# Two layers and a routed block on one core: norm factors applied at the products' exit

## The chip, the cores and the metric

The kernel runs on one core of a Trainium2 chip, as one program. The metric is device microseconds of that core for the whole program, the median of several runs; smaller is better. TensorE multiplies, VectorE and ScalarE prepare its operands and take its results out of PSUM, GpSimd does part of the expert stage, and SyncE's queue issues the transfers of weights.

## What is computed

The input is x, 512 tokens by 1024, and all is fp32. Two layers are followed by a second block:

```python
for l in range(2):
    x = x + 0.5 * swiglu(rmsnorm(x, ffn1_norm[l]), w_gate, w_up, w_down)
    h = rmsnorm(x, mix_norm[l])
    parts = split(h @ w_in[l])
    o = concat(mla_attention(...), nsa_attention(...), stick_breaking_attention(...))
    x = x + o @ w_out[l]
    x = x + 0.5 * swiglu(rmsnorm(x, ffn2_norm[l]), w_gate, w_up, w_down)
x = rmsnorm(x, final_norm)
hn = rms_norm(x, attn_norm_g)
h = x + (sigmoid(ga) * (gmlp(u, v) @ w_proj_a) + sigmoid(gb) * (swa(q, k, v) @ w_proj_b)) @ w_out
h = h + hierarchical_moe(rms_norm(h, ffn_norm_g), ...)   # 16 experts, two for each token
out = rms_norm(h, final_norm_g)
```

`rmsnorm(x, g)` is x · g · rstd, with rstd = (mean of x² over the 1024 features + eps)^(−1/2), one factor for each token. `swiglu` is (silu(h w_gate) · (h w_up)) w_down with 2816 inner columns, silu(a) = a · sigmoid(a).

## The kernel before

**Layout and products.** x stays on chip transposed, `x_T`: 8 chunks (`KC`) of 128 features by 512 tokens. Each matrix product is done in split form: an operand is rounded to a high part (`..._hi`, ScalarE) and the remainder is its low part (`..._lo`, VectorE), and hi·hi, lo·hi and hi·lo are summed in PSUM. One such product is 128 × 128 by 512 columns.

**Feed-forward parts** (`slices`, two in each layer). The 2816 inner columns go in `NSL` = 11 slices of 256. In a slice TensorE does the gate half (48 products, into `score[0:2]`), the up half (48, `score[2:4]`) and the down part of an earlier slice (8 chunks `c` of 6 products, into two banks `acc[c % 2]` in turn), whose results VectorE adds to `x_T`. The weights of each half go through `split_weights(l, ph, w, sl)` on ScalarE and then on VectorE, w = 0 for gate, 1 for up, 2 for down. The gate half is turned into silu by ScalarE's Exp of −a and VectorE's add of 1, reciprocal and product (`gate`); `hidden` multiplies by the up half and splits the result. The last slice's down weights are put into the gate weights' tiles (`tile=0`).

**Norms** (`norm` on TensorE and ScalarE, `square_sum` and `norm_split` on VectorE). As each chunk of x becomes final (`x_final`), ScalarE squares it into `h_T` and VectorE sums the squares. Two fp32 products with a matrix of ones sum over the partitions (`ssq_full`). ScalarE computes rstd with Ln and Exp, VectorE writes x · gain · rstd into `h_T`, ScalarE makes its high part and VectorE its low part, chunk by chunk. Then the first products of the next stage can run.

**Mixer** (`mix`). A list of tickets `MIX` (name, number, weight load, evacuating engine) sets the order; each has one product group from `acc[n % 2]`, and the engine in the list takes the result out. After the attentions come the tickets of the output product: p0 to p7 (first 768 rows of w_out), then q0 to q7 (last 256 rows, unsplit fp32), whose results VectorE adds to x. Loads of weights share three slots in turn; a load is issued when the last ticket that uses its slot is done (`LAST_TICKET`), and the next part's gate weights take slot 0.

**Second block.** Its own norm (`norm_both`), then tickets `SEC_T`: u, v, wst (transposes of the spatial weights), q, k, values, the sliding window attention with half of a gate ticket in each step, and so on to the router. **Experts** (`step`, `x_pass`): for each of 16, ScalarE makes the high parts, VectorE the low parts of the gate and up weights in two pieces each (`xg_lo`, `xu_lo`) and of the expert's gathered tokens (`mine_lo`), and GpSimd those of the down weights (`xd_lo`, line 2682). TensorE does gate, up and an earlier expert's down half in turn.

Each engine works through its own instructions in the order in which the code writes them; an instruction that waits holds up all behind it on its engine.

## Time and profile before

| | |
|---|---|
| time, median of 3 runs | 3158.56 us (3156.81 to 3162.05) |
| profiled execution | 3159.24 us |
| its span | 3157.4 us |
| mean granted TensorE clock | 0.965 |
| TensorE busy | 2927.1 us, 93% |
| VectorE busy | 2042.9 us, 65% |
| ScalarE busy | 1136.5 us, 36% |
| GpSimd busy | 217.3 us, 7% |

The span is that of one profiled execution; the times of the runs are taken without a profile. A timeline row has its start, its duration, engine, line, operation, output and inputs, and in brackets how long the engine stood idle before it and what ended that. Rows with "x2" are two instructions taken together. A matrix product's duration of 0.39 us is that at the granted clock of 2.4 GHz, 0.63 and more at 1.2 GHz; the starts of such products in a run lie closer than their durations, since they overlap.

### The profile page before, as it was taken

What the parts mean: (1) busy time and instruction counts of PE and PEld (TensorE: products, weight loads), DVE (VectorE), ACT (ScalarE), POOL (GpSimd) and SP (SyncE); (2) the same over time, 40 slices, a digit from 0 to 9 for tenths busy, and PEclk for the clock granted to TensorE, in tenths of its full rate; (3) what the DMA queues carried; (4) which work ended last, traced back from release to release, by engine and by line L of the source; (5) the groups of instructions that cost most, each with busy time, mean ns of one, the idle gap of its engine ahead of it and who ended that gap; (6) DMA issues with size and microseconds to landing.
All of it is one profiled execution on the core that took longest, in us unless ns stands there. A gap on an engine that the chain in (4) does not pass through costs nothing. (4 is left out here: it accounts for less than half of the span.)

```text
span 3157.4 us, 36951 instructions
## 1 busy us (share of the span) xinstructions
PE 2927.1 (93%) x13178; PEld 2257.2 (71%) x13178; DVE 2042.9 (65%) x2675; ACT 1136.5 (36%) x1658; POOL 217.3 (7%) x68
## 2 busy tenths in 40 slices
PE   5999989999899998999989999899997999978885
PEld 3888868566588886888767566588876767667774
DVE  5677742675577777777733774677776544467876
ACT  3212132467321213221132566322114333256674
POOL 0000000000000000000000000000000000046663
PEclk8999999999999999999999999999998889989998
DMA  6323223000232322232232000323214112368995
GB/s 160 107 93 99 89 63 75 31 1 24 80 107 93 102 84 81 93 106 93 78 75 63 21 1 24 107 93 106 93 40 116 55 43 79 132 229 319 326 337 195
DMA packets 234685, 324.56 MB, mean 103 GB/s; under 512 B 58720, under 2 KB 202088, under 8 KB 222144
## 3 DMA queue, kind: packets, MB, share of 16 engines
q1 hardware_dynamic: 228400, 309.88, 30.3%
q0 software_dynamic: 5584, 11.02, 1.3%
q10 hardware_dynamic: 576, 2.10, 0.2%
q8 instruction: 65, 1.06, 0.1%
q14 instruction: 60, 0.49, 0.0%
...
## 5 line engine op out<-in xcount | busy, mean ns | idle before, releaser
L2024 DVE SCALAR_TENSOR_TENSOR x_T<-acc,x_T 128x512 f32<-128x512 f32 x352 | 242.9, 691 | 205.3 <-PE acc L929 205.3
L898 PE MATMUL score<-h_hi,gate_hi 128*128 128x512 f32 x704 | 280.2, 398 | 41.5 <-DVE h_lo L1978 32.5
L2004 DVE RECIPROCAL recip_tile<-exp_tile 128x512 f32<-128x512 f32 x88 | 295.1, 3353 | 7.2 <-issue 0.9
L899 PE MATMUL score<-h_lo,gate_hi 128*128 128x512 f32 x704 | 278.4, 396 | 0.0
L900 PE MATMUL score<-h_hi,gate_lo 128*128 128x512 f32 x704 | 278.2, 395 | 0.0
L898 PE MATMUL score<-h_hi,up_hi 128*128 128x512 f32 x704 | 274.6, 390 | 0.1
L900 PE MATMUL score<-h_hi,up_lo 128*128 128x512 f32 x704 | 274.2, 390 | 0.0
L899 PE MATMUL score<-h_lo,up_hi 128*128 128x512 f32 x704 | 274.2, 390 | 0.0
L927 PE MATMUL acc<-hid_hi,down_hi 128*128 128x512 f32 x640 | 251.9, 394 | 8.8 <-DVE x_T L2024 8.8
L928 PE MATMUL acc<-hid_lo,down_hi 128*128 128x512 f32 x640 | 252.0, 394 | 0.0
L929 PE MATMUL acc<-hid_hi,down_lo 128*128 128x512 f32 x640 | 251.9, 394 | 0.0
L1514 ACT ACTIVATE up_hi<-weights 128x2048 fp32r<-128x2048 f32 x44 | 84.4, 1918 | 311.0 <-PE score L900 310.0
L1514 ACT ACTIVATE down_hi<-weights 128x2048 fp32r<-128x2048 f32 x40 | 76.7, 1917 | 327.3 <-PE acc L929 326.8
L898 PEld LDWEIGHTS score<-h_hi,gate_hi 128*128 128x128 f32 x704 | 135.1, 192 | 76.0 <-DVE h_lo L1978 37.2
L1592 ACT ACTIVATE exp_tile<-score 128x512 f32<-128x512 f32 x88 | 47.8, 595 | 367.9 <-PE score L900 367.9
L2667 POOL DMA_DIRECT2D arena<-rel_scratch x1 | 1.0, 964 | 2375.9 <-PE acc L1252 2375.9
L2569 DVE TENSOR_TENSOR xg_lo<-arena,xg_hi 128x2048 fp32r<-128x2048 f32 x32 | 127.8, 4024 | 50.6 <-ACT xg_hi L1854 50.6
L899 PEld LDWEIGHTS score<-h_lo,gate_hi 128*128 128x128 f32 x704 | 135.2, 192 | 28.1
L900 PEld LDWEIGHTS score<-h_hi,gate_lo 128*128 128x128 f32 x704 | 134.8, 191 | 28.5
L2682 POOL TENSOR_TENSOR xd_lo<-weights,xd_hi 128x2048 fp32r<-128x2048 f32 x30 | 154.2, 5163 | 5.7 <-ACT xd_hi L1854 5.3
L898 PEld LDWEIGHTS score<-h_hi,up_hi 128*128 128x128 f32 x704 | 132.2, 188 | 28.7 <-issue 0.9
L899 PEld LDWEIGHTS score<-h_lo,up_hi 128*128 128x128 f32 x704 | 132.2, 188 | 27.3
...
## 6 DMA issues: line engine op xcount, KB each, us to landing
...
```

What stands on the lines that cost most here:

```text
L898: mm(ps, hi[:, kc, cols], h_hi[:, kc, :], start=kc == 0, stop=False, skip_group_check=True)
L899: mm(ps, hi[:, kc, cols], h_lo[:, kc, :], start=False, stop=False, skip_group_check=True)
L900: return mm(ps, lo[:, kc, cols], h_hi[:, kc, :], start=False, stop=kc == KC - 1, skip_group_check=True)
L927: mm(acc[c % 2][:, :], hi[:, j, cols], hid_hi[:, 2 * par + j, :], start=j == 0, stop=False)
L928: mm(acc[c % 2][:, :], hi[:, j, cols], hid_lo[:, 2 * par + j, :], start=False, stop=False)
L929: m = mm(acc[c % 2][:, :], lo[:, j, cols], hid_hi[:, 2 * par + j, :], start=False, stop=j == 1)
L1514: fn(w_hi[tile][:, :], slot[w][:, :], ACT.Copy).then_inc(w_hi_ready[w], 1)
L1592: fn(et[:, c, :], score[c][:, :], ACT.Exp, scale=-1.0).then_inc(sig_ready, 1)
L2004: V.reciprocal(rt[:, :], et[:, c, :])
L2024: V.scalar_tensor_tensor(x_T[:, c, :], acc[c % 2][:, :], 0.5, x_T[:, c, :], ALU.mult, ALU.add).then_inc(acc_free[c % 2], 1)
L2569: V.tensor_tensor(x_lo[t][j][:, :], x_raw[t][j], x_hi[t][j][:, :], ALU.subtract).then_inc(x_lo_ready[t], 1)
L2682: nc.gpsimd.tensor_tensor(x_lo["d"][j][:, :], x_raw["d"][j], x_hi["d"][j][:, :], ALU.subtract).then_inc(x_lo_ready["d"], 1)
```

## The change

1. **Norm factors at the exit.** In both layers the split is made of x · gain (`enter` on ScalarE, `low` on VectorE), with no rstd in it. The rstd of a token is multiplied in when a product leaves PSUM: in `gate` two products by rstd (`gated`), and two more (`gated2`) that carry the up half's factor; in the mixer in the evacuations, which for that move from ScalarE to VectorE, and for the two by-token kinds (vsw, sv) with a transposed copy `rstd_T`.
2. **Square sums behind products.** VectorE adds the squares up (`add_squares`), and TensorE's products with ones (`sum_squares`) stand between gate and up half of slice 0, and in the mixer ahead of the second ticket.
3. **Tangent for the sigmoid.** ScalarE computes tanh(a/2), VectorE (tanh + 1) · gated2; the factor of down becomes 0.25. The reciprocals go, and `gate_taken` is given after the first two products by rstd.
4. **Reorderings.** (a) The loads of w_out change slots, q's with p's last, so that slot 0 is free after p7, and the gate weights of the second part are split ahead of the q adds. (b) wst comes first in the second block. (c) The sliding window's half gate products come one step earlier. (d) In the experts `mine_lo` comes between the two `xg_lo`. Besides, the last slice's down weights go into the tiles of gate or up (`tile=ph`) and wait until the last up half is done, and the mixer's first weights are split ahead of the last adds of the first part.

```diff
-    [("cq", 0, 0, "act"), ("cq", 1, 0, "act"), ("ckv", 0, 1, "act"), ("kr", 0, 1, "act")]
...
+    [("cq", 0, 0, "dve"), ("cq", 1, 0, "dve"), ("ckv", 0, 1, "dve"), ("kr", 0, 1, "dve")]
...
+    + [("sq", 0, 7, "dve"), ("rope", 10, None, "dve"), ("sq", 1, 7, "dve"), ("xs_v", 0, None, "act")]
...
-for _n in range(W_OUT0, W_OUT0 + 4):
-    LAST_TICKET[_n] = OUT_T["p", 2 * (_n - W_OUT0) + 1]
-LAST_TICKET[W_OUT0 + 4] = OUT_T["q", KC - 1]
+P_LOAD, Q_LOAD = (14, 15, 16, 18), 17
+for _j, _n in enumerate(P_LOAD):
+    LAST_TICKET[_n] = OUT_T["p", 2 * _j + 1]
+LAST_TICKET[Q_LOAD] = OUT_T["q", KC - 1]
...
-        SEC_T = ([("u", c, c // 2) for c in range(4)]
+        SEC_T = ([("wst", b, None) for b in range(2)]
+                 + [("u", c, c // 2) for c in range(4)]
                  + [("v", b, 2 + b // 2) for b in range(4)]
-                 + [("wst", b, None) for b in range(2)]
...
+            def sum_squares(k, sq, n_direct):
+
+                for c in range(KC - n_direct, KC):
+                    pe.wait_ge(squared, k * KC + c + 1)
+                    mm(turn[0][:, :], cst("ones"), sq[c], start=c == KC - n_direct, stop=False)
...
                 pe.wait_ge(summed, k + 1)
-                mm(turn[0][:, :], cst("ones"), h_T[:, 0, :], start=True, stop=False)
-                pe.wait_ge(squared, k * KC + KC)
-                mm(turn[0][:, :], cst("ones"), h_T[:, KC - 1, :], start=False, stop=True).then_inc(ssq_full, 1)
+                mm(turn[0][:, :], cst("ones"), sums, start=False, stop=True).then_inc(ssq_full, 1)
...
                     half(sl, 0)
+                    if isinstance(sl, int) and sl == 0:
+                        sum_squares(l * 3 + 2 * ph, ffn_sq, 1)
                     half(sl, 1)
...
-                    tile = 0 if last else 2
+                    tile = ph if last else 2
...
+                    if (name, i) == ("cq", 1):
+                        sum_squares(l * 3 + 1, mix_sq, 2)
+                    if (name, i) == ("nq", 1):
+                        pe.wait_ge(rstd_ready, l * 3 + 2)
+                        for b in range(TB):
+                            m = nc.tensor.transpose(turn[1][:, b * P:(b + 1) * P], rstd[:, b * P:(b + 1) * P], ident)
+                        m.then_inc(rstd_turned, 1)
...
+                half_gate(0)
...
-                    g = n // 2
-                    linear2(T2["gate", g], "gate", g, 7 + g // 2, range(4 * (n % 2), 4 * (n % 2) + 4))
+                    if n + 1 < NSW:
+                        half_gate(n + 1)
...
+            def row_scale(k):
+
                 act.wait_ge(ssq_full, k + 1)
                 fn(rstd[:, :], turn[0][:, :], ACT.Ln, scale=1.0 / D, bias=eps[:, :])
                 act.drain()
                 fn(rstd[:, :], rstd[:, :], ACT.Exp, scale=-0.5).then_inc(rstd_ready, 1)
...
+            def enter(k, sq, hi):
+
+                for c in range(KC):
+                    act.wait_ge(x_final, k * KC + c + 1)
+                    fn(hi[:, c, :], x_T[:, c, :], ACT.Copy, scale=gains[:, bass.ds(k, 1), c:c + 1][:, 0, :]
+                       ).then_inc(h_hi_ready, 1)
+                    fn(sq[c], x_T[:, c, :], ACT.Square).then_inc(squared, 1)
...
+                    if not later:
+                        row_scale(l * 3 + 2 * ph)
                     act.wait_ge(hid_done, at(l, TG, gub + sl * 2 + 2))
-                    act.wait_ge(gu_full, gu_at(l, gub, sl * 2 + 1))
+                    act.wait_ge(gate_taken, slices_at(l, ph, sl + 1))
                     for c in range(2):
-                        fn(et[:, c, :], score[c][:, :], ACT.Exp, scale=-1.0).then_inc(sig_ready, 1)
+                        fn(et[:, c, :], gated[c], ACT.Tanh, scale=0.5).then_inc(sig_ready, 1)
...
-                split_weights(l, ph, 2, NSL - 1, tile=0)
+                act.wait_ge(gu_full, gu_at(l, gub, 2 * NSL))
+                split_weights(l, ph, 2, NSL - 1, tile=ph)
...
-                norm(l * 3 + 1, mix=l)
+                split_mix(l, 0)
+                enter(l * 3 + 1, mix_sq, mix_h[0])
                 mix(l)
-                norm(l * 3 + 2, (l, 1))
+                split_weights(l, 1, 0, 0)
+                enter(l * 3 + 2, ffn_sq, h_hi)
...
+            def low(l, nth, c):
+
+                hi, lo = mix_h if nth == 1 else (h_hi, h_lo)
+                dve.wait_ge(h_hi_ready, at(l, 3 * KC, nth * KC + c + 1))
+                V.scalar_tensor_tensor(lo[:, c, :], x_T[:, c, :], gains[:, bass.ds(l * 3 + nth, 1), c:c + 1][:, 0, :],
+                                       hi[:, c, :], ALU.mult, ALU.subtract).then_inc(h_split, 1)
+
+            def add_squares(k, sq, n, out=sums):
+
+                dve.wait_ge(squared, k * KC + n)
+                m = V.tensor_tensor(out, sq[0], sq[1], ALU.add)
+                for c in range(2, n):
                     dve.drain()
-                    dve.wait_ge(h_hi_ready, at(l, 3 * KC, nth * KC + c + 1))
-                    V.tensor_tensor(lo[:, c, :], h_T[:, c, :], hi[:, c, :], ALU.subtract).then_inc(h_split, 1)
-
-                if ph is None:
-                    split_mix(l, 0)
-                else:
-                    split_weights(l, ph, 0, 0)
-                dve.wait_ge(rstd_ready, k + 1)
-                for c in range(KC):
-                    V.scalar_tensor_tensor(h_T[:, c, :], x_T[:, c, :], gains[:, bass.ds(k, 1), c:c + 1][:, 0, :],
-                                           rstd[:, :], ALU.mult, ALU.mult).then_inc(h_ready, 1)
-                    if c >= 1:
-                        low(c - 1)
-                low(KC - 1)
-                if ph is None:
-                    split_mix(l, 1)
-
-            def slices(l, ph, k):
+                    m = V.tensor_tensor(out, out, sq[c], ALU.add)
+                m.then_inc(summed, 1)
...
+                    if isinstance(sl, int) and sl == 0:
+                        dve.wait_ge(rstd_ready, l * 3 + 2 * ph + 1)
+                    dve.wait_ge(gu_full, gu_at(l, gub, sl * 2 + 1))
                     for c in range(2):
+                        m = V.tensor_tensor(gated[c], score[c][:, :], rstd[:, :], ALU.mult)
+                    m.then_inc(gate_taken, 1)
+                    dve.drain()
+                    for c in range(2):
+                        V.tensor_tensor(gated2[c], gated[c], rstd[:, :], ALU.mult)
+                    for c in range(2):
+                        dve.drain()
                         dve.wait_ge(sig_ready, at(l, TG, gub + sl * 2 + c + 1))
-                        V.tensor_scalar(et[:, c, :], et[:, c, :], 1.0, None, ALU.add)
-                        dve.drain()
-                        V.reciprocal(rt[:, :], et[:, c, :])
-                        dve.drain()
-                        m = V.tensor_tensor(et[:, c, :], rt[:, :], score[c][:, :], ALU.mult)
-                    m.then_inc(gate_taken, 1)
+                        V.scalar_tensor_tensor(et[:, c, :], et[:, c, :], 1.0, gated2[c], ALU.add, ALU.mult)
...
-                        V.scalar_tensor_tensor(x_T[:, c, :], acc[c % 2][:, :], 0.5, x_T[:, c, :],
+                        V.scalar_tensor_tensor(x_T[:, c, :], acc[c % 2][:, :], 0.25, x_T[:, c, :],
...
                         if last:
                             dve.drain().then_inc(x_final, 1)
-                            square_sum(k, c - 1)
+                            if ph == 0 and c >= 1:
+                                low(l, 1, c - 1)
...
-                split_weights(l, ph, 2, NSL - 1, tile=0)
+                split_weights(l, ph, 2, NSL - 1, tile=ph)
...
+                if ph == 0:
+                    split_mix(l, 0)
                 down(NSL - 1, True)
...
             def mix(l):
+                low(l, 1, KC - 1)
+                add_squares(l * 3 + 1, mix_sq, KC - 2)
+                split_mix(l, 1)
...
+                    if (name, i) == ("cq", 0):
+                        dve.wait_ge(rstd_ready, l * 3 + 2)
+                    if who == "dve" and (name, i) in EVAC:
+                        t, sc = EVAC[name, i]
+                        r = t.shape[0]
+                        V.scalar_tensor_tensor(t, ps[0:r, :], sc, rstd[0:r, :], ALU.mult, ALU.mult
+                                               ).then_inc(acc_free[n % 2], 1)
...
+                split_weights(l, 1, 0, 0)
                 dve.drain()
                 for c in range(KC):
                     add_out("q", c)
                     dve.drain().then_inc(x_final, 1)
-                    square_sum(l * 3 + 2, c - 1)
+                    if c >= 1:
+                        low(l, 2, c - 1)
+                low(l, 2, KC - 1)
+                add_squares(l * 3 + 2, ffn_sq, KC - 1)
...
-                    split_x("g", n + 1)
+                    split_x("g", n + 1, (0,))
                     mine_split(n + 1, 1 - q)
+                    split_x("g", n + 1, (1,))
```

VectorE at the end of the first feed-forward part, before: the hidden split of the last slice, adds to x of the two last down parts (L2024), sums of squares into h_T (L1953), then the mixer's first weight split.

```order
L2014 TENSOR_TENSOR exp_tile<-exp_tile,score 128x512 x2
L2016 CAST hid_hi<-exp_tile 128x1024
L2018 TENSOR_TENSOR hid_lo<-exp_tile,hid_hi 128x1024
...
L2024 SCALAR_TENSOR_TENSOR x_T<-acc,x_T 128x512
...
L2024 SCALAR_TENSOR_TENSOR x_T<-acc,x_T 128x512
...
L1953 TENSOR_TENSOR h_T<-h_T 128x512
...
L2024 SCALAR_TENSOR_TENSOR x_T<-acc,x_T 128x512
...
L1967 TENSOR_TENSOR mix_w_lo_62<-weights,mix_w_hi_61 128x2048
```

The same place after. L2066 is the add to x, L2012 the mixer's weight split, L2019 the low part of x · gain, L2025 and L2028 the sums of squares.

```order
L2056 TENSOR_TENSOR exp_tile<-exp_tile,score 128x512 x2
L2058 CAST hid_hi<-exp_tile 128x1024
L2060 TENSOR_TENSOR hid_lo<-exp_tile,hid_hi 128x1024
...
L2066 SCALAR_TENSOR_TENSOR x_T<-acc,x_T 128x512
...
L2012 TENSOR_TENSOR mix_w_lo_62<-weights,mix_w_hi_61 128x2048
...
L2066 SCALAR_TENSOR_TENSOR x_T<-acc,x_T 128x512
...
L2019 SCALAR_TENSOR_TENSOR mix_h_lo<-x_T,gains,mix_h_hi 128x512
...
L2066 SCALAR_TENSOR_TENSOR x_T<-acc,x_T 128x512
...
L2025 TENSOR_TENSOR probs_T<-arena 128x512
L2028 TENSOR_TENSOR probs_T<-probs_T,arena 128x512 x4
```

The weight split has moved ahead of the last eight adds, the low parts between them, and the sums behind them.

VectorE in the q tickets of the mixer, before: the last p add, q adds (L2215), sums of squares, and behind them the split of the second part's gate weights (L1961) and the norm.

```order
L2215 TENSOR_TENSOR x_T<-acc,x_T 128x512
...
L2215 TENSOR_TENSOR x_T<-acc,x_T 128x512
...
L1953 TENSOR_TENSOR h_T<-h_T 128x512
...
L2215 TENSOR_TENSOR x_T<-acc,x_T 128x512
...
L1961 TENSOR_TENSOR gate_lo<-weights,gate_hi 128x2048
...
L1986 SCALAR_TENSOR_TENSOR h_T<-x_T,gains,rstd 128x512
...
L1978 TENSOR_TENSOR h_lo<-h_T,h_hi 128x512
```

The same place after.

```order
L2271 TENSOR_TENSOR x_T<-acc,x_T 128x512
...
L2006 TENSOR_TENSOR gate_lo<-weights,gate_hi 128x2048
...
L2271 TENSOR_TENSOR x_T<-acc,x_T 128x512
...
L2019 SCALAR_TENSOR_TENSOR h_lo<-x_T,gains,h_hi 128x512
...
L2271 TENSOR_TENSOR x_T<-acc,x_T 128x512
...
L2025 TENSOR_TENSOR probs_T<-h_T 128x512
L2028 TENSOR_TENSOR probs_T<-probs_T,h_T 128x512 x5
```

The split of gate_lo now stands between the last p add and the first q add, and low parts follow each q add.

VectorE in one expert's step, before.

```order
L2569 TENSOR_TENSOR xg_lo_65<-arena,xg_hi_71 128x2048
...
L2569 TENSOR_TENSOR xg_lo_66<-arena,xg_hi_72 128x2048
L2576 TENSOR_TENSOR mine_lo_79<-turn,mine_hi_77 128x512 x2
L2593 SCALAR_TENSOR_TENSOR probs<-recip_tile,score 128x512
...
L2596 SCALAR_TENSOR_TENSOR probs<-probs,score 128x512
L2569 TENSOR_TENSOR xu_lo_67<-arena,xu_hi_73 128x2048
```

The same step after.

```order
L2636 TENSOR_TENSOR xg_lo_65<-arena,xg_hi_71 128x2048
L2643 TENSOR_TENSOR mine_lo_79<-turn,mine_hi_77 128x512
...
L2636 TENSOR_TENSOR xg_lo_66<-arena,xg_hi_72 128x2048
L2661 SCALAR_TENSOR_TENSOR probs<-recip_tile,score 128x512
...
L2664 SCALAR_TENSOR_TENSOR probs<-probs,score 128x512
L2636 TENSOR_TENSOR xu_lo_67<-arena,xu_hi_73 128x2048
```

The second xg_lo has moved behind mine_lo; the rest stands as it did.

## Rows read from the trace of the kernel before

**Rows 1.** The page, part 1: busy us, share of the span, instructions.

```profile
PE 2927.1 (93%) x13178; PEld 2257.2 (71%) x13178; DVE 2042.9 (65%) x2675; ACT 1136.5 (36%) x1658; POOL 217.3 (7%) x68
```

**Rows 2.** The page, part 5: line, operation, count, busy us, mean ns, idle before.

```profile
L2004 DVE RECIPROCAL recip_tile<-exp_tile 128x512 f32<-128x512 f32 x88 | 295.1, 3353 | 7.2 <-issue 0.9
```

**Rows 3.** Timeline of TensorE: start us, us, line, operands, [idle before, its releaser].

```profile
72.11 0.79 PE L898 MATMUL score<-h_hi,gate_hi 128*128 128x512 f32 x1 [5.57 <-DVE gate_lo L1961]
...
400.85 0.50 PE L927 MATMUL acc<-hid_hi,down_hi 128*128 128x512 f32 x1 [2.19 <-DVE x_T L2024]
...
418.80 1.92 PE L878 MATMUL turn<-h_T,const 128*128 128x512 f32 x2 [2.25 <-DVE h_T L1953]
...
427.60 0.80 PE L949 MATMUL acc<-mix_h_hi,mix_w_hi 128*128 128x512 f32 x1 [5.18 <-DVE mix_h_lo L1978]
...
438.38 0.39 PE L949 MATMUL acc<-mix_h_hi,mix_w_hi 128*128 128x512 f32 x1
438.61 0.40 PE L949 MATMUL acc<-mix_h_lo,mix_w_hi 128*128 128x512 f32 x1
...
825.93 1.13 PE L878 MATMUL turn<-h_T,const 128*128 128x512 f32 x2 [1.68 <-DVE h_T L1953]
...
837.93 0.80 PE L898 MATMUL score<-h_hi,gate_hi 128*128 128x512 f32 x1 [10.02 <-DVE h_lo L1978]
...
863.37 0.49 PE L898 MATMUL score<-h_hi,gate_hi 128*128 128x512 f32 x1 [1.19 <-DVE gate_lo L1961]
...
1216.35 0.80 PE L898 MATMUL score<-h_hi,gate_hi 128*128 128x512 f32 x1 [5.20 <-DVE h_lo L1978]
...
2392.74 0.77 PE L1252 MATMUL acc<-mix_h_hi,sec_hi 128*128 128x512 f32 x1 [13.82 <-DVE mix_h_lo L2344]
...
2449.14 0.80 PE L1252 MATMUL acc<-mix_h_hi,sec_hi 128*128 128x512 f32 x1 [5.19 <-DVE exp_tile L2493]
...
2494.93 1.22 PE L1306 MATMUL score<-arena 64*128 64x256 f32 x2 [4.06 <-DVE stats L2436]
...
2952.45 0.49 PE L1417 MATMUL score<-xg_hi,mine_hi 128*128 128x512 f32 x1 [2.25 <-DVE mine_lo L2576]
```

**Rows 4.** Timeline of VectorE, end of the first feed-forward part and mixer.

```profile
389.40 2.29 DVE L1961 TENSOR_TENSOR gate_lo<-weights,gate_hi 128x2048 fp32r<-128x2048 f32 x1
...
391.89 0.69 DVE L2024 SCALAR_TENSOR_TENSOR x_T<-acc,x_T 128x512 f32<-128x512 f32 x1 [0.20 <-PE acc L929]
...
430.51 0.74 DVE L1986 SCALAR_TENSOR_TENSOR h_T<-x_T,gains,rstd 128x512 f32<-128x512 f32 x1
...
514.07 2.08 DVE L2159 SCALAR_TENSOR_TENSOR lora<-lora,lora_gains,exp_tile 128x512 f32<-128x512 f32 x3
```

**Rows 5.** Timeline of ScalarE, first norm of the mixer, gate weights of the second part.

```profile
422.46 0.69 ACT L1562 ACTIVATE rstd<-turn,eps 128x512 f32<-128x512 f32 x1 [0.80 <-PE turn L880]
...
424.50 0.63 ACT L1564 ACTIVATE rstd<-rstd 128x512 f32<-128x512 f32 x1
...
829.57 1.91 ACT L1514 ACTIVATE gate_hi<-weights 128x2048 fp32r<-128x2048 f32 x1 [3.89 <-DMA weights<-in_ffn_w_gate]
```

**Rows 6.** Windows in the mixer: stretch, us, busy of PE, PEld, DVE, ACT, POOL, clock, DMA.

```profile
480.00:525.00 45.00, 43.64 (x240) 36.30 (x239) 15.62 (x15) 18.50 (x21) 0.00 (x0) 1.00 0.44 94
```

**Rows 7.** Timeline of VectorE, one expert.

```profile
2942.62 8.49 DVE L2569 TENSOR_TENSOR xg_lo<-arena,xg_hi 128x2048 fp32r<-128x2048 f32 x2 [3.03 <-ACT xg_hi L1854]
...
2951.03 1.28 DVE L2576 TENSOR_TENSOR mine_lo<-turn,mine_hi 128x512 fp32r<-128x512 f32 x2
...
2953.68 4.49 DVE L2569 TENSOR_TENSOR xu_lo<-arena,xu_hi 128x2048 fp32r<-128x2048 f32 x2
```

**Rows 8.** Timeline of GpSimd, two experts.

```profile
2936.40 10.36 POOL L2682 TENSOR_TENSOR xd_lo<-weights,xd_hi 128x2048 fp32r<-128x2048 f32 x2
...
2956.86 5.78 POOL L2682 TENSOR_TENSOR xd_lo<-weights,xd_hi 128x2048 fp32r<-128x2048 f32 x1
```

**Rows 9.** Line 2682 on GpSimd: duration ns min/median/max.

```profile
L2682 POOL TENSOR_TENSOR xd_lo<-weights,xd_hi x30: 4595/4633/6666, 2809.1 to 3106.5; 128x2048 fp32r<-128x2048 f32 x30
```

142 lines of the change are left out of this document (79 added, 63 removed).

## The prediction, made before the changed kernel had run

> **What bounds the kernel now.** I read the page's busy shares first: TensorE is busy for 2927.1 of 3157.4 us [rows 1]. Whatever does not take away an idle stretch of TensorE, or put work into one, moves nothing. So the second view is TensorE's timeline, and in it the rows that end an idle stretch [rows 3]. They stand where one stage hands over to the next: at each norm, at the end of each feed-forward part, in the second block's first steps, and once for each expert. The third view is the timelines of VectorE and ScalarE at these places [rows 4, 5], to see which instruction ends each wait and what is queued ahead of it. The last views are VectorE's and GpSimd's timelines in the experts [rows 7 to 9]. The sum is made against the profiled execution's own 3159.24 us, which lies 0.7 above the median of 3158.56.
>
> **What frees an engine but not the path.** The tangent takes away 88 reciprocals of 3.35 us, 295 us of VectorE [rows 2]. VectorE is at 65% [rows 1]. Inside the slices TensorE does not wait for it, so I book 0. The cover is the next slice's split weights, which are ready some 9 us before they are used: VectorE's split of gate_lo starts at 389.40 [rows 4], and in every slice comes ahead of eight down chunks of 1.36 us.
>
> **Start.** The first products come about 3 us sooner, since no norm precedes them. But TensorE then stops again where it stops now, at 72.11, for gate weights whose transfer the change does not touch [rows 3]. 0, bounds ±1.5.
>
> **First feed-forward part into the mixer (twice).** Before, the last down product ends at 418.80 − 2.25 = 416.55. The two square-sum products, the Ln and the Exp (422.46 to 425.13 [rows 5], with a table load between them), and gain and factor on VectorE lie before 427.60. The first ticket then runs at 1.2 GHz (0.80 us a record against 0.39 at 438.38) and waits chunk by chunk; the second ticket begins at 438.38 [rows 3]. After the change, new things come first. The last down weights are split only when the up half of the last slice is done, so ScalarE's 1.9 and VectorE's 2.29 stand ahead of the add that now starts at 391.89 [rows 4]: +2.3. The mixer's first weight split (2.29) is put ahead of the last adds, where TensorE has two banks of 1.36 of cover: +1.0. VectorE then needs about 1.56 per chunk (add 0.69, the low part 0.75 [rows 4], a drain) against TensorE's 1.36: +0.9. So down ends at 420.8, and the first ticket follows without a wait, 24 products 0.227 apart (438.38, 438.61 [rows 3]) = 5.4, to 426.2. Three fp32 products of 0.86 (the pair at 825.93 takes 1.13 with its run-out [rows 3]) bring it to 428.8. The chain of squares (last low part, five adds of 0.69) ends near 426.4 and is covered with little to spare. 438.4 − 428.8 = 9.6 saved, bounds 7 to 12, twice: **−19.2**.
>
> **Inside the mixer.** Fifteen evacuations per layer go from ScalarE (0.60) to VectorE (0.75, as the row with gain and factor [rows 4]). TensorE has two banks and tickets of some 5.5 us, and VectorE is busy for only 15.6 of 45 us there [rows 6]. Only the one behind the short gate ticket is late: VectorE is in the lora products until 516.15 [rows 4], so that the ticket after next starts some 1.55 later. Four transposes add 0.6, and one wait of 0.5 goes. 1.65 twice: **+3.3**, bounds 1 to 6.
>
> **Mixer into the second feed-forward part (twice).** Before, the gate weights could be requested only behind the last q chunk (825.93 − 1.68 = 824.2) and their ScalarE split starts at 829.57 [rows 3, 5], 5.3 later; TensorE starts at 837.93 after 10.02 idle. Now they are requested when p7 is done, at 810.5, and land at 815.9; ScalarE has its part at 817.8 and VectorE at 820.1. But VectorE's split is written ahead of all q adds, so the two banks are full at 813.9 and TensorE stands until 820.9: a **new wait of 7.0**. Six q chunks of 1.72 follow, some 3 us slower since the clock falls in such a gap as it does at 427.60. q ends at 834.2, and the gate half starts at once. At full clock (10.9, and 1.7 for two square products) the up half begins at 846.8, where it now begins at 851.0. The wait of 1.19 at 863.37 [rows 3], behind VectorE's reciprocals, goes too. 5.4 twice: **−10.8**. Bounds: 0, if the new wait costs all that it hides, and 8.
>
> **Second feed-forward part into layer 1.** The same late split (+2.3). The norm's 11.1 us between down and gate half become 3.9 of low parts and gate_lo, and two square products of 1.7 inside. The slow start after the 5.20 at 1216.35 [rows 3] shrinks by 1, and slice 1 no longer waits (1.2). **−4.6**, bounds 2 to 7.
>
> **Into the second block.** Its norm stays; the wait of 13.82 at 2392.74 [rows 3] hangs on weights requested after the last x, so it follows the late split: +1.6. The spatial transposes (1.35) move into it, with the 5.19 wait at 2449.14 that they caused [rows 3], and the slow ticket behind that wait gets 2.1 back: **−7.0**, bounds 4 to 9.
>
> **Sliding window.** Half a gate product (12 products, 2.75) is moved into the wait of 4.06 at 2494.93 [rows 3], and part of the slow clock with it goes: −4.7, +0.4 at the next ticket: **−4.3**, bounds 1 to 6.
>
> **Experts.** TensorE idles 2.25 before nearly each gate half, released by mine_lo [rows 3]. The change puts mine_lo ahead of the second xg_lo (2.28), which looks like −2.2 for each of 15 experts, −33. The rows speak against it. xg_lo's pair takes 8.49 where two of 2.28 would take 4.6 [rows 7]: the first starts at 2942.62, while GpSimd's xd_lo runs until 2946.76 [rows 8], and ends 2.15 after that. GpSimd's pair takes 10.36 [rows 8] where two of the median 4.63 [rows 9] would take 9.3: it is issued at 2956.86, and VectorE's xu_lo pair runs until 2958.17 [rows 7]. The two engines exclude each other, and their turns form a ring: from the end of xd_lo VectorE needs 11.4 (xg_lo twice, mine_lo, two short ones, xu_lo twice, 2946.76 to 2958.17 [rows 7]), then GpSimd 9.2, together 20.5; the two xd_lo starts lie 20.46 apart [rows 8]. The change only permutes three members of this ring. TensorE starts each gate half 2.2 sooner and waits 2 us longer for xd_lo in the down half: **0**, bounds ±4: the longest xd_lo took 6.7 [rows 9], 2 us lost in the ring, and two such may come or go.
>
> The Trainium skill's page "SBUF — State Buffer", section "Who interferes with whom", says that a VectorE instruction with two SBUF inputs and a GpSimd one that reads SBUF hold a shared port by an exclusive lock, the later one blocked for the whole of the earlier. By that rule the experts give 0; by a mere sharing of bandwidth they would give up to −33. The trace agrees with the rule: 2.15 us after xd_lo's end is one whole xg_lo.
>
> **Sum.** 0 − 19.2 + 3.3 − 10.8 − 4.6 − 7.0 − 4.3 + 0 = −42.6. 3159.24 − 42.6 = 3116.6, and 0.7 less on the median: **3116**. All the favourable bounds together give −67, the others −10.
>
> **The rivals.** (1) *New waits eat the gain.* The 7.0 before the q adds saves nothing, and each of the four late down splits costs 4.6 and not 2.3, as TensorE falls to the lower clock behind them: −42.6 + 10.8 + 9.2 = −22.6, 3136; with the mixer's bound, 3139. For it: the idle of 7.0 is longer than the 5.18 after which the clock is low at 427.60 [rows 3]. Against: weights and q adds have nothing else ahead of them. (2) *The ring in the experts opens.* If xu_lo and xd_lo interleave so that VectorE's 2.7 us of unlocked work hides behind GpSimd, each cycle falls towards TensorE's own 18.2 (20.46 − 2.25): up to −33, about 3083. Against: 11.4 and 9.2 make up the 20.46 to 0.2 us, and the order of xu_lo and xd_lo is not changed. (3) *Slower than before: VectorE becomes the mixer's exit.* If each of the 30 moved evacuations stands behind a weight split of 2.29 when its bank is needed, the mixer costs 68.7 instead of 3.3: −45.9 + 68.7 = +23, 3181. It is slower than before from 1.7 us each. Against: a late evacuation costs only what exceeds the second bank's 5.5 us, and VectorE is one third busy there [rows 6]. (4) *The change does not do what it says:* the sum products wait on TensorE for squares that come too late (they lie 2 us ahead), so that TensorE stands between first and second ticket, as now before the first. The three norm terms (−34.6) go and what they had absorbed (4.2 twice, 2.3) stays: −42.6 + 34.6 + 10.7 = +2.7, 3161, no change.
>
> **How the numbers follow.** Forecast, 3092 to 3140 with rival 1's smaller forms: 0.80. Rival 1 beyond 3140: 0.07. Rival 2 below 3092: 0.04. Rival 4, within 0.2% (6.3 us, about what a measurement of this kernel can tell from none): 0.04. Rival 3 and like ones, slower: 0.05. Faster by more than 0.2%: 0.91, same 0.04, slower 0.05. The range is that of the 0.80.
>
> **What would show it.** In the trace after: no idle before the first mixer ticket, and the second beginning some 9.6 us sooner counted from the end of the up half of the last slice; a new wait near 7 us in the q chunks with gate_lo as releaser, and none before the gate half; in the experts still 20.5 between xd_lo pairs, with TensorE's wait moved from mine_lo to xd_lo. A ring below 20 would prove the experts' step wrong; waits at mixer tickets released by VectorE's evacuations, of more than 1 us and more than two a layer, would prove the mixer's.

## The result, and the profile after

The changed kernel takes 3127.02 us, the median of four runs (3123.23 to 3128.6), against 3158.18 for the kernel before in the same session: a ratio of 0.9898 (95% interval 0.9882 to 0.9914), 31.2 us less. The forecast was 3116, with a range from 3092 to 3140. In a second session it took 3129.42, and the kernel before 3161.63 (0.9906, 0.9891 to 0.9921). Its profiled execution took 3123.23 and is the shortest of its four runs; its span is 36.0 below that of before.

The page of the changed kernel, head and part 1:

```profile
span 3121.4 us, 36929 instructions
...
PE 2920.3 (94%) x13194; PEld 2256.0 (72%) x13194; DVE 1825.3 (58%) x2653; ACT 1121.3 (36%) x1638; POOL 212.4 (7%) x68
```

TensorE's idle time fell from 230 to 201 us; VectorE lost 218 us of work. The timeline of TensorE after, rows that end an idle stretch or begin a stage:

```profile
395.12 0.50 PE L940 MATMUL acc<-hid_hi,down_hi 128*128 128x512 f32 x1 [2.30 <-DVE x_T L2066]
...
420.32 0.49 PE L962 MATMUL acc<-mix_h_hi,mix_w_hi 128*128 128x512 f32 x1
...
425.90 1.88 PE L889 MATMUL turn<-arena,const 128*128 128x512 f32 x4
...
428.07 0.79 PE L962 MATMUL acc<-mix_h_hi,mix_w_hi 128*128 128x512 f32 x1
...
507.18 0.50 PE L962 MATMUL acc<-mix_h_hi,mix_w_hi 128*128 128x512 f32 x1 [1.82 <-DVE arena L2199]
...
813.18 12.68 PE L954 MATMUL acc<-o_T,weights 128*128 128x512 f32 x24 [7.09 <-DVE x_T L2271]
...
1200.33 0.79 PE L909 MATMUL score<-h_hi,gate_hi 128*128 128x512 f32 x1 [6.89 <-DVE h_lo L2019]
...
2366.76 0.77 PE L1271 MATMUL acc<-mix_h_hi,sec_hi 128*128 128x512 f32 x1 [11.11 <-DVE mix_h_lo L2412]
```

These answer to [rows 3]. 420.32 is the first mixer ticket: the waits of 2.25 and 5.18 at 418.80 and 427.60 are gone, and 428.07 is the second ticket, which began at 438.38. Its first record overlaps the sums ahead of it, so the table below goes by its second product (428.70 after, 438.61 before). 395.12 and 813.18 are the two waits that the prediction added (2.3 and 7.0 forecast, 2.30 and 7.09 found). 1200.33 answers to the row at 1216.35, and its wait has grown from 5.20 to 6.89. At 2366.76 the second block's wait is 11.11 where it was 13.82, since the spatial transposes and two more products with ones fill part of it.

Where the 36.0 us of the two profiled executions lie, read at the same instruction of TensorE in both timelines (start after minus start before, and the difference between neighbouring places):

| place | ahead of before by | this stretch | forecast |
|---|---|---|---|
| up to the first part's last down products | 0.4 | −0.4 | 0 |
| mixer's second ticket, layer 0 | 9.9 | −9.5 | −9.6 |
| first q chunk, layer 0 | 7.9 | +2.0 | +1.65 |
| slice 1 of the second part, layer 0 | 14.1 | −6.2 | −5.4 |
| slice 1 of the first part, layer 1 | 16.7 | −2.6 | −4.6 |
| mixer's second ticket, layer 1 | 25.9 | −9.2 | −9.6 |
| first q chunk, layer 1 | 21.6 | +4.3 | +1.65 |
| slice 1 of the second part, layer 1 | 27.8 | −6.2 | −5.4 |
| first row of the sliding window | 34.7 | −7.0 | −7.0 |
| first expert's gate half | 39.9 | −5.2 | −4.3 |
| end | 36.0 | +3.9 | 0 |

### The profile page after: what moved, and what is told of

Same layout as the page of the kernel before. It is cut to its first block, busy times and chain, and to the rows that moved or that the text cites. A ratio compares the mean times of both kernels' runs of the same rounds, so it can differ in the third digit from the quotient of the medians.

```text
span 3121.4 us, 36929 instructions
## 1 busy us (share of the span) xinstructions
PE 2920.3 (94%) x13194; PEld 2256.0 (72%) x13194; DVE 1825.3 (58%) x2653; ACT 1121.3 (36%) x1638; POOL 212.4 (7%) x68
## 4 chain that ended last, share of the span: by engine, by line
PE 83%; DVE 4%; DMA 3%; issue 2%; ACT 2%; POOL 2%; DVEq 1%; SPq 1%; ACTq 0%; POOLq 0%
PE score L909 10%; PE score L911 10%; PE score L910 10%; PE acc L1271 8%; PE acc L962 6%; PE acc L940 5%; PE acc L942 5%; PE acc L941 5%; PE score L996 4%; PE acc L1017 4%; PE score L1444 3%; POOL xd_lo L2750 2%; PE acc L1444 2%; PE acc L954 2%; DMA weights<-in_ffn_w_gate 1%
## 5 line engine op out<-in xcount | busy, mean ns | idle before, releaser
L2066 DVE SCALAR_TENSOR_TENSOR x_T<-acc,x_T 128x512 f32<-128x512 f32 x352 | 242.4, 691 | 402.8 <-PE acc L942 402.4
L909 PE MATMUL score<-h_hi,gate_hi 128*128 128x512 f32 x704 | 277.7, 394 | 22.1 <-DVE h_lo L2019 14.1
L1620 ACT ACTIVATE exp_tile<-probs 128x512 f32<-128x512 f32 x88 | 50.8, 625 | 409.1 <-DVE probs L2041 409.1
L940 PEld LDWEIGHTS acc<-hid_hi,down_hi 128*128 128x128 f32 x640 | 120.9, 189 | 46.3 <-DVE x_T L2066 21.3
```

The lines of the kernel that those rows point to most:

```text
L909: mm(ps, hi[:, kc, cols], h_hi[:, kc, :], start=kc == 0, stop=False, skip_group_check=True)
L940: mm(acc[c % 2][:, :], hi[:, j, cols], hid_hi[:, 2 * par + j, :], start=j == 0, stop=False)
L2066: V.scalar_tensor_tensor(x_T[:, c, :], acc[c % 2][:, :], 0.25, x_T[:, c, :], ALU.mult, ALU.add).then_inc(acc_free[c % 2], 1)
```

## The experiments

Each kernel was timed against the kernel before on the same chip. "−n" is the median's distance from that kernel's. "Less than the changed kernel" goes by the median of the changed kernel's second session, 3129.42.

**The changed kernel again (`a0_after`).** No edit.

> The changed kernel once more, unaltered, as the measure for the runs beside it. Its profiled execution was 36.0 us below that of the kernel before, the medians 31.2 apart. Expected: 3127 again, within 3; where two executions differ, the difference should lie in the experts (from about 2746 us to the end), where the distance between two pairs of xd_lo is irregular (19.3 to 22.5), and not ahead of them.

Measured 3129.42 (3125.8 to 3134.5), −32.2. Its trace is 0.35 ahead of the first one's at the start, loses 2.2 more than that one in layer 0's mixer, stays 2.2 to 2.5 behind up to the experts and ends 2.6 behind. So the difference lies in the mixer and not, as I had expected, in the experts (+4.1 here, +3.9 there, though their pairs of xd_lo lie differently); more on that below.

**The experts' order undone (`e1_moe_undo`).**

```diff
-                    split_x("g", n + 1, (0,))
+                    split_x("g", n + 1)
                     mine_split(n + 1, 1 - q)
-                    split_x("g", n + 1, (1,))
```

> The changed kernel with the experts' order as before (both xg_lo, then mine_lo). Theory of the ring (VectorE's and GpSimd's instructions exclude each other, and their turns set the distance of 20.5): the reordering gains nothing and by the traces loses 3 to 4 us (39.9 us ahead at the first expert's gate half, 36.0 at the end), so this kernel takes 3122 to 3125. Rival (TensorE's wait on mine_lo was the bound, and the reordering saves what it moves): this kernel is slower than the changed one by 5 to 30.

Measured 3124.76 (3123.43 to 3128.06), −36.9, ratio 0.9889 (0.9874 to 0.9904) where the changed kernel has 0.9906 (0.9891 to 0.9921). The medians are 4.7 apart in the forecast direction, with overlapping intervals. The rival that the reordering saves 5 to 30 us falls. The traces say less than the medians: from the first gate half to the end this kernel is 4.1 longer than before, which has the same order there, and the changed one 3.9 and 4.1 in its two traces. So the 3.9 can't be put down to the order. The length of this stage differs without any edit in it: with the old order it is 3.1 longer than before in `f1_tanh_only` and 0.1 in `f2_wst_half`, with the new order 6.4 in `e2_gatelo_late` and 8.1 in `e5_unroll`. What the reordering costs by itself lies between nothing and 5 us; it was not settled. That it gains nothing by itself is shown.

**An expert's two products ahead of the first xg_lo (`e3_probs_first`).**

```diff
+                dve.wait_ge(xsig_ready, n + 1)
+                V.scalar_tensor_tensor(xhid, sig, 1.0, score[q][:, :], ALU.add, ALU.mult)
+                dve.drain()
+                dve.wait_ge(x_used["u"], n * 2 + 4)
+                V.scalar_tensor_tensor(xhid, xhid, 0.5, score[2 + q][:, :], ALU.mult, ALU.mult).then_inc(xhid_ready, 1)
                 if last is None:
                     split_x("g", n + 1, (0,))
...
-                dve.wait_ge(xsig_ready, n + 1)
```

> The changed kernel with VectorE's two products of one expert's gate and up results (0.67 and 0.69, with 0.15 between) moved ahead of the first xg_lo. They read PSUM, so that they can run while GpSimd does xd_lo. Theory of the ring: 1.5 us less in each of 14 rounds of it, 21 in all, so 3106, with 19.0 between xd_lo pairs. Rival (transfers bound this stage; their engines are 0.9 busy at some 330 GB/s): within 5 of the changed kernel. Second rival: VectorE waits there for the up half, misses xd_lo's end, and it is slower by up to 10.

Measured 3111.42 (3105.94 to 3112.88), −50.2: 18.0 less than the changed kernel beside it. GpSimd's timeline in it:

```profile
2914.63 9.18 POOL L2750 TENSOR_TENSOR xd_lo<-weights,xd_hi 128x2048 fp32r<-128x2048 f32 x2
...
2934.67 9.18 POOL L2750 TENSOR_TENSOR xd_lo<-weights,xd_hi 128x2048 fp32r<-128x2048 f32 x2
...
2954.71 4.63 POOL L2750 TENSOR_TENSOR xd_lo<-weights,xd_hi 128x2048 fp32r<-128x2048 f32 x1
```

The distance of pairs (from end to end), 20.5 or 21.5 in eleven of the fourteen rounds of the kernel before, is 20.0 to 20.1 in eleven and 19.0 in the last three. The forecast was 19.0, and 21 us in all. GpSimd's gather is now what stands between: it ends 0.9 after xu_lo, so that a round is 10.0 of VectorE, 0.9 and 9.2 of xd_lo.

**The same edit on the kernel before (`f3_before_probs`).**

> The kernel before with one change alone: VectorE's two products of an expert's gate and up results ahead of the first xg_lo. Theory of the ring: its rounds of 20.5 and 21.5 (20.8 on average) become 20.0, so 11 to 18 less than before, by the experts alone, with no other stage touched. Rival: the gain of e3 came from the place of mine_lo in it, and this kernel gains under 4.

Measured 3159.28 (3157.02 to 3165.35), ratio 1.0001 (0.9992 to 1.001): no gain at all. Here my theory of the ring fell short: it had VectorE's splits and GpSimd's xd_lo in it, but not the two indirect transfers that GpSimd issues ahead of each xd_lo: the store of an expert's result (L2686) and the gather of a later expert's tokens (L2674). Two rounds of this kernel, VectorE, then GpSimd, then TensorE:

```profile
2973.51 4.48 DVE L2569 TENSOR_TENSOR xu_lo<-arena,xu_hi 128x2048 fp32r<-128x2048 f32 x2
...
2987.09 0.69 DVE L2593 SCALAR_TENSOR_TENSOR probs<-probs,score 128x512 f32<-128x512 f32 x1 [3.56 <-PE score L1417]
...
2993.55 4.48 DVE L2569 TENSOR_TENSOR xu_lo<-arena,xu_hi 128x2048 fp32r<-128x2048 f32 x2
```

```profile
2974.81 1.87 POOL L2686 DMA_INDIRECT expert_scratch<-exp_tile,slot_ids  x1 [6.78 <-ACT exp_tile L1871]
2976.98 1.88 POOL L2674 DMA_INDIRECT lora<-h_scratch,slot_ids  x1 [0.31 <-issue]
2978.88 9.19 POOL L2682 TENSOR_TENSOR xd_lo<-weights,xd_hi 128x2048 fp32r<-128x2048 f32 x2
2996.13 2.78 POOL L2686 DMA_INDIRECT expert_scratch<-probs_T,slot_ids  x1 [8.06 <-ACT probs_T L1871]
2999.22 1.00 POOL L2674 DMA_INDIRECT lora<-h_scratch,slot_ids  x1 [0.30 <-issue]
3000.24 9.20 POOL L2682 TENSOR_TENSOR xd_lo<-weights,xd_hi 128x2048 fp32r<-128x2048 f32 x2
```

```profile
2973.73 0.49 PE L1417 MATMUL score<-xg_hi,mine_hi 128*128 128x512 f32 x1 [2.59 <-DVE mine_lo L2576]
...
2993.76 0.49 PE L1417 MATMUL score<-xg_hi,mine_hi 128*128 128x512 f32 x1 [0.22 <-DVE mine_lo L2576]
```

The product at 2987.09 waits for the up half (idle 3.56, released by TensorE), so VectorE's row of instructions now hangs on TensorE too. Still the pace is that of the ring through GpSimd. From the end of xd_lo at 2968.02 VectorE needs 10.0 up to the end of xu_lo (2977.99), where it needed 11.4 before. The gather ends 0.9 later, xd_lo takes 9.2: together 20.1. In the next round, from 2988.07, the store starts later against xu_lo. Now it is the store that ends 0.9 after xu_lo (2998.03 and 2998.91), and the gather comes on top with 1.3: 21.4. The pairs lie 20.1 and 21.4 apart by turns, where they lay 20.5 and 21.5 apart in most rounds of the kernel before. So the two issues ate most of the 1.5 that the move took off VectorE, and two rounds of 23.0 and 23.4 ate the rest.

The same place in the kernel with both edits (`e3_probs_first`), VectorE, then GpSimd's store and gather:

```profile
2898.97 0.69 DVE L2660 SCALAR_TENSOR_TENSOR probs<-probs,score 128x512 f32<-128x512 f32 x1 [1.72 <-PE score L1444]
...
2899.57 6.36 DVE L2636 TENSOR_TENSOR xg_lo<-arena,xg_hi 128x2048 fp32r<-128x2048 f32 x1
...
2905.85 1.28 DVE L2643 TENSOR_TENSOR mine_lo<-turn,mine_hi 128x512 fp32r<-128x512 f32 x2
...
2907.05 2.27 DVE L2636 TENSOR_TENSOR xg_lo<-arena,xg_hi 128x2048 fp32r<-128x2048 f32 x1
```

```profile
2909.90 2.52 POOL L2754 DMA_INDIRECT expert_scratch<-probs_T,slot_ids  x1 [6.13 <-ACT probs_T L1916]
2912.72 1.89 POOL L2742 DMA_INDIRECT lora<-h_scratch,slot_ids  x1 [0.30 <-issue]
```

Here mine_lo ends at 2907.13, ahead of the second xg_lo, and the gate half starts 3.5 after the end of xd_lo, not 5.7. The down half ends 3.1 after it in all rounds but the first, as in the short rounds of `f3_before_probs`; in the long ones there it ends 5.3 to 5.5 after it. The store waits until ScalarE has taken out the down half, and in this kernel it is always early enough. This points to a way from mine_lo's place to GpSimd through TensorE. ScalarE's queue, which waits for weights as well, stands between the two, and what share it has in the store's moment was not tested. By the medians, the reordering in the change is worth nothing alone, the two products' move is worth nothing alone, and together they take 18 us.

**The gate weights' split behind q6 (`e2_gatelo_late`).**

```diff
-                split_weights(l, 1, 0, 0)
                 dve.drain()
                 for c in range(KC):
+                    if c == 7:
+                        split_weights(l, 1, 0, 0)
                     add_out("q", c)
```

> The changed kernel with VectorE's split of the second part's first gate weights between the q6 and q7 adds, not ahead of q0's. Theory (the new wait of 7.1 at the q chunks is only the price of that place): q chunks run without a stop, the split ends near 817.5 where the gate half now starts at 825.3, so 7 to 8 us less in each layer, 3112. Rival (ScalarE's and VectorE's work chunk by chunk or the lower clock behind the norm sets the start of the gate half): less than 3 in each layer.

Measured 3119.5 (3117.45 to 3122.52), −42.1, 9.9 less than the changed kernel. Slice 1 of the second part starts 9.7 ahead of before, counted from the first q chunk, in each layer, where the change gives 6.2: 3.5 each and not 7 to 8. ScalarE's timeline, then TensorE's:

```profile
808.74 1.91 ACT L1541 ACTIVATE gate_hi<-weights 128x2048 fp32r<-128x2048 f32 x1 [9.06 <-DMA weights<-in_ffn_w_gate]
...
810.55 0.70 ACT L1591 ACTIVATE h_hi<-x_T,gains 128x512 fp32r<-128x512 f32 x1
```

```profile
812.82 7.13 PE L954 MATMUL acc<-o_T,weights 128*128 128x512 f32 x16 [2.58 <-DVE x_T L2271]
...
822.87 0.49 PE L909 MATMUL score<-h_hi,gate_hi 128*128 128x512 f32 x1 [2.91 <-DVE gate_lo L2006]
```

ScalarE stands 9.06 us in front of the transfer, and only at 810.55 makes the first high part, of a chunk that had been ready since 804. VectorE's low part of that chunk, written between two q adds, waits for it, and TensorE stands at 812.82.

**Both splits in the middle of the q chunks (`e8_gate_mid`).** ScalarE's stands behind its third chunk, VectorE's ahead of the q6 add.

```diff
             def enter(k, sq, hi, split=None):
                 for c in range(KC):
+                    if split is not None and c == 3:
+                        split_weights(split, 1, 0, 0)
...
                 for c in range(KC):
+                    if c == 6:
+                        split_weights(l, 1, 0, 0)
                     add_out("q", c)
```

> As e2_gatelo_late, but ScalarE's split of the gate weights stands behind its third chunk of x, and VectorE's between the q5 and q6 adds. In e2 ScalarE's queue stood in front of a transfer that had not landed, its high parts came late, and VectorE, which makes the low part between two q adds, came late with them (2.6 us of idle in the q chunks and 2.9 ahead of the gate half). Theory: both go, the gate half starts near 817 to 818, and the time is 10 to 12 less than e2's in both layers together, 19 to 22 less than the changed kernel's. Rival: two banks do not cover a split of 2.29 in the middle of chunks of 1.72, and 2 us a layer stay.

Measured 3114.78 (3109.64 to 3122.22), −47.0, 14.6 less than the changed kernel, with a wide spread. Timeline of VectorE, then of TensorE:

```profile
814.27 2.28 DVE L2007 TENSOR_TENSOR gate_lo<-weights,gate_hi 128x2048 fp32r<-128x2048 f32 x1
```

```profile
816.69 0.49 PE L909 MATMUL score<-h_hi,gate_hi 128*128 128x512 f32 x1 [0.87 <-DVE gate_lo L2007]
```

The gate half starts at 816.69 after 0.87 of idle (the q chunks run without a stop), where it started at 825.29. From the first q chunk to slice 1 this kernel gains 14.6 on before in layer 0 and 14.7 in layer 1, 17 more than the change. The median shows 14.6 of it.

**No wait for the last up half (first part) (`e4_no_up_wait`).**

```diff
-                act.wait_ge(gu_full, gu_at(l, gub, 2 * NSL))
+                if ph == 1:
+                    act.wait_ge(gu_full, gu_at(l, gub, 2 * NSL))
                 split_weights(l, ph, 2, NSL - 1, tile=ph)
+                if ph == 0:
+                    act.wait_ge(gu_full, gu_at(l, gub, 2 * NSL))
```

> The changed kernel, where the last slice's down weights of the first part of each layer are split without waiting for the last up half; ScalarE waits for that half behind the split instead. Theory: the wait of 2.3 at the third down chunk (395.1 and 1546.0) is that wait's price alone, so it goes in both layers and the time falls by 4 to 5 against the changed kernel. Rival: VectorE, whose low parts and adds need 1.56 a chunk, is then the limit of the last down part, and more than half of the 2.3 comes back there.

Measured 3117.24 (3114.96 to 3119.49), −44.6, 12.2 less than the changed kernel; 4 to 5 were forecast. TensorE's first idle in these down parts is now the old one:

```profile
400.13 0.66 PE L940 MATMUL acc<-hid_hi,down_hi 128*128 128x512 f32 x1 [2.19 <-DVE x_T L2069]
```

Up to the second mixer ticket it gains 2.3 more than the change in layer 0 (−11.8 against −9.5, from the same place) and 2.6 in layer 1, 5 in all, as forecast; it leads the changed kernel by 4.3 at the sliding window and by 3.7 or 6.3 at the end, by which of its two traces is taken. The median's other 6 or 7 us are in no stretch of the traces, and stay open.

**VectorE's layers written out (`e5_unroll`).**

```diff
-            with dve.Fori(0, DEPTH) as l:
+            for l in range(DEPTH):
```

> The changed kernel with VectorE's loop over the two layers written out, so that it does not jump back. Its only other difference is that addresses with the layer's number are constants. Theory: of the wait of 6.9 ahead of layer 1's gate half some 3 us are VectorE's idle after the jump, which no semaphore ends; they go, and the time falls by 3 to 4. Rival: the wait is that for ScalarE's or the transfer's part of the gate weights, and nothing changes (within 1).

Measured 3120.28 (3116.36 to 3123.45), −41.5, 9.1 less than the changed kernel. VectorE's row for gate_lo in the changed kernel, then in this one, then TensorE's start of the gate half in this one:

```profile
1197.32 2.29 DVE L2006 TENSOR_TENSOR gate_lo<-weights,gate_hi 128x2048 fp32r<-128x2048 f32 x1 [3.15 <-issue]
```

```profile
1191.65 2.29 DVE L2006 TENSOR_TENSOR gate_lo<-weights,gate_hi 128x2048 fp32r<-128x2048 f32 x1
```

```profile
1194.66 0.50 PE L909 MATMUL score<-h_hi,gate_hi 128*128 128x512 f32 x1 [3.88 <-DVE h_lo L2019]
```

The idle of 3.15 that no semaphore ended is gone, and TensorE's wait is 3.88 instead of 6.89. The stretch gives −7.0 instead of −2.6, 4.4 more, 3.0 of them in this wait. Another 2.8 lie in the mixer (the two layers together, against the first trace of the changed kernel), which the edit was not meant to touch. In the experts this trace loses 4.2 more than that one, so that it ends only 3.3 ahead of it; the median's 9.1 are not accounted for stretch by stretch.

**The tangent alone (`f1_tanh_only`).** The kernel before with this:

```diff
-                        fn(et[:, c, :], score[c][:, :], ACT.Exp, scale=-1.0).then_inc(sig_ready, 1)
+                        fn(et[:, c, :], score[c][:, :], ACT.Tanh, scale=0.5).then_inc(sig_ready, 1)
...
-                        V.tensor_scalar(et[:, c, :], et[:, c, :], 1.0, None, ALU.add)
-                        V.reciprocal(rt[:, :], et[:, c, :])
-                        m = V.tensor_tensor(et[:, c, :], rt[:, :], score[c][:, :], ALU.mult)
+                        m = V.scalar_tensor_tensor(et[:, c, :], et[:, c, :], 1.0, score[c][:, :], ALU.add, ALU.mult)
```

> The kernel before with the tangent for the sigmoid alone: no reciprocals, one VectorE instruction for three, factor 0.25 for 0.5. Theory: 88 reciprocals (295 us of VectorE) hide beside TensorE except in slice 0, where the first split of the next gate weights stands behind them: the waits of 1.19 to 1.26 and 1.00 at the second slices go, 4 us less than before at most. Rival: VectorE's 295 us bind more than the timeline shows, 10 us or more less.

Measured 3153.13 (3149.7 to 3156.8), ratio 0.9976 (0.9965 to 0.9986), 8.7 less than before. Its trace leads by 6.6 at the first expert, more than the 4 that I allowed: 1.4 at slice 1 of the second part, 3.7 up to slice 1 of layer 1, 1.7 up to the next mixer; layer 1's mixer loses 2.6, and the stages behind it give 3.0. Some 4 are the waits of the second slices, as forecast; the rest is not explained by a wait that I could name. Of VectorE's 295 us at most the 8.7 bound.

**Two reorderings alone (`f2_wst_half`).** The kernel before with wst first (`SEC_T` and its evacuation within the norm) and the half gates one step earlier.

```diff
-        SEC_T = ([("u", c, c // 2) for c in range(4)]
+        SEC_T = ([("wst", b, None) for b in range(2)]
+                 + [("u", c, c // 2) for c in range(4)]
...
+                half_gate(0)
                 scores(2)
```

> The kernel before with two of the reorderings alone: the spatial transposes first in the second block (VectorE takes them out within the norm, whose second factor lies in another tile), and the half gate products one step earlier. Theory, by the traces of before and after: 7 less at the first row of the sliding window and 5 less after it, 12 in all ahead of the experts. Rival: the last 5 belong to the norm's change and only 7 come.

Measured 3148.18 (3143.52 to 3150.26), ratio 0.9962 (0.9948 to 0.9976), 11.9 less than before. The trace gains 8.9 up to the sliding window's first row and 4.9 after it. In the changed kernel the first of these is 7.0; the 1.9 between them have the size of the late split of the last down weights. The second belongs to the half gates, not to the norms. By the medians, the tangent and these two reorderings alone make 20.6 of the change's 31.2. The norm factors at the exit were not timed without them.

**All that helped, and the same with the experts' old order.** `e9_all` has the edits of e3, e8, e4 and e5 together; `e10_all_undo` differs from it by the diff of e1.

> The changed kernel with all that helped: the products ahead of the first xg_lo (e3), the gate weights' split in the middle of the q chunks (e8), no wait for the last up half (e4), VectorE's layers written out (e5). If the terms are independent, they add: 18 + 17 + 5 + 4 = 44 less than the changed kernel, 3085. If the experts give a part back, since they start at another moment against the transfers, 3090 to 3095.

> As e9_all, with the experts' xg_lo pair together as in the kernel before, mine_lo behind it. Theory of the ring: the same time as e9_all within 2, since mine_lo only changes places in it. Rival: mine_lo's place matters once the ring is shorter, since TensorE's own 18.2 comes nearer: then this kernel is 5 or more slower.

Measured 3081.53 (3079.17 to 3083.2) and 3094.57 (3089.12 to 3095.35), ratios 0.9748 (0.9735 to 0.9762) and 0.9792 (0.9779 to 0.9806). The first is 78.6 less than the kernel before, where the changed kernel is 31.2 and 32.2 less, so 46 to 47 less than that one, where 44 were forecast from the stretches of the traces. (The medians of the four single edits add up to 54.) It is the fastest version of this study. The second is 13 us slower, and the traces place this in the experts: from the first gate half to the end e9_all gains 11.1 on before, e10_all_undo 1.3. Its pairs lie 20.1 and 21.4 apart by turns, as in `f3_before_probs`, those of e9_all mostly 20.0. That contradicts what I expected from a ring of the splits alone; the rival, that mine_lo's place matters once the ring is shorter, came.

## Why the prediction was right, and where its steps were off

The forecast's direction, its range and its main terms held: 3116 against 3127, 42.6 forecast, 36.0 in the profiled execution and 31.2 in the medians. That the total of the profiled execution comes within 7 is in part luck: the terms of the mixer, of layer 1 and of the experts fell short by 8.9 together, and others gave some 2 more than forecast.

- **Start:** right. TensorE's second wait still ends at 72.14; it has grown from 5.57 to 8.04.
- **First part into the mixer:** right, −9.5 and −9.2 for −9.6. All four parts of it are there: the wait of 2.30 at 395.12; 0.55 at 410.95 and not 1.0 for the mixer's split; the down part longer by what VectorE needs; no wait at the first ticket. The square sums were ready in time: the four instructions at 425.90 follow the ticket without idle.
- **Mixer:** the mechanism was right (one wait behind the gate ticket, 1.82 for 1.55 at 507.18), the size off in layer 1: +4.3 for +1.65. The missing 2.3 lie between the compression's wait (3.30, in both kernels) and the first scores, and they are a matter of the clock. Two stretches there, after, with columns as in [rows 6]:

```profile
1736.00:1746.00 10.00, 8.09 (x25) 5.12 (x26) 5.97 (x19) 3.85 (x14) 0.00 (x0) 0.50 0.17 60
...
1746.00:1756.00 10.00, 10.00 (x48) 6.36 (x47) 6.24 (x21) 5.31 (x17) 0.00 (x0) 0.84 0.00 0
```

  The eighth number, the granted clock, is 0.50 and 0.84: at 1.2 GHz TensorE spends the whole of the first stretch and a part of the next. In the kernel before the corresponding stretches 1760 to 1770 and 1770 to 1780 have 0.66 and 1.00. Over the ten traces of kernels with the changed mixer it costs 1.5 to 2.1 in six of twenty layers, 3.6 to 4.5 in thirteen and 5.9 in one; in the kernel with the tangent alone, whose mixer is that of before, layer 1's costs 2.6 more than before. The other five layers of the kernels with the mixer of before (`f1_tanh_only`, `f2_wst_half`, `f3_before_probs`) are within 0.2 of it. So the changed mixer comes into the slow stretch far more often, and its usual cost is nearer +4 than +1.65. Why is not shown, and I had left it out of the range's reasons.
- **Mixer into the second part:** −6.2 for −5.4. The new wait was 7.09 for 7.0; the q chunks after it lost 1.8 to the slow clock and not 3. Rival 1 (it saves nothing) fell.
- **Into layer 1:** −2.6 for −4.6, the clearest miss. I let VectorE begin gate_lo as soon as its last add was done, 3.9 us of idle for TensorE. In fact VectorE stood 3.15 us at the loop's jump, and TensorE 6.89. In the kernel before VectorE stood 2.33 there, and ScalarE's split, which it waited for, ended only 0.7 before it went on, so the jump lay mostly beneath that wait. The step that failed is the count of what stood behind the removed wait. `e5_unroll` gives 3.88. Besides, the items of this term as written (+2.3, −11.1, +3.9, +1.7, −1, −1.2) add up to −5.4 and not to −4.6; with 3.0 more for the wait that is −2.4.
- **Second block and sliding window:** −7.0 for −7.0, −5.2 for −4.3.
- **Experts:** 0 forecast, +3.9 in the profiled execution, at the edge of the ±4. That the order of xg_lo and mine_lo gives nothing was right, and `e1_moe_undo` confirms it. TensorE's waits moved as the prediction said. Its waits before, total, times and longest:

```profile
PE score L1417 <- DVE mine_lo L2576: 33.6, 16, 4.3
...
PE acc L1417 <- POOL xd_lo L2682: 3.7, 6, 1.5
```

  The same after:

```profile
PE acc L1444 <- POOL xd_lo L2750: 21.3, 10, 3.5
...
PE score L1444 <- DVE mine_lo L2643: 7.3, 9, 2.7
PE score L1444 <- DVE xu_lo L2636: 6.8, 2, 3.4
```

  The 20.5 was less regular than the prediction had it. Of the fourteen rounds before, seven take 20.5; four take 21.5, and in these the gather ends 0.9 after xu_lo; the others 19.3, 20.3 and 22.5. After, they go from 18.1 to 22.5. Timelines of GpSimd, VectorE and TensorE after:

```profile
2831.87 12.52 POOL L2750 TENSOR_TENSOR xd_lo<-weights,xd_hi 128x2048 fp32r<-128x2048 f32 x2
...
2856.67 9.18 POOL L2750 TENSOR_TENSOR xd_lo<-weights,xd_hi 128x2048 fp32r<-128x2048 f32 x2
```

```profile
2831.02 8.88 DVE L2636 TENSOR_TENSOR xu_lo<-arena,xu_hi 128x2048 fp32r<-128x2048 f32 x2
...
2840.43 6.10 DVE L2636 TENSOR_TENSOR xg_lo<-arena,xg_hi 128x2048 fp32r<-128x2048 f32 x1
...
2859.57 8.44 DVE L2636 TENSOR_TENSOR xg_lo<-arena,xg_hi 128x2048 fp32r<-128x2048 f32 x1 [1.16 <-ACT xg_hi L1899]
```

```profile
2839.96 0.50 PE L1444 MATMUL score<-xu_hi,mine_hi 128*128 128x512 f32 x1 [3.41 <-DVE xu_lo L2636]
```

  At 2831.87 GpSimd is issued while VectorE's first xu_lo runs and takes the turn ahead of the second, which then needs 6.7 of the pair's 8.88; TensorE waits 3.41 for it. The prediction named this interleaving as rival 2 and let it save time; here it cost about as much as it saved, and the mean distance of pairs stayed 20.8, as before. At the first expert alone 3.2 us are lost: 2.0 where an xg_lo slipped in between the two xd_lo (6.6 for the second), most of the rest because ScalarE's xd_hi came later. Since the kernel with the order undone loses 4.1 as well, in other places, the order is not shown to be the cause of the 3.9.
- **Exclusion of VectorE and GpSimd:** the long xu_lo begun at 2833.2 ends 2.2 after GpSimd's instruction (2831.87 + 5.89), one whole duration of its own, and the long xd_lo ends 4.5, about one of its own, after xu_lo. The Trainium skill's page "SBUF — State Buffer", section "Who interferes with whom", says that a VectorE instruction with two SBUF inputs and a GpSimd one that reads SBUF contend for an exclusive lock, which the earlier holds to its end; the trace agrees. What the prediction lacked are GpSimd's store and gather as members of the ring: they cost 0.9 or 2.2 in a round of `f3_before_probs`.
- **Rivals 3 and 4** did not come: no evacuation in the mixer by VectorE but the named one delays TensorE by as much as 1 us (the other is 0.44 in each layer), and TensorE waits nowhere for the square sums. Rival 3's 1.7 us for each evacuation is where the kernel becomes measurably slower; it is slower from 1.5 (45.9 over 30).

The rest between 36.0 and 31.2 is the choice of execution: the profiled one was the shortest of its kernel's, while the profiled one of before, 3159.24, was 1.1 above the median of 3158.18.
